# A decoder block on one core: the FFN factor spread by DMA, its squares between the high parts, and one attention product moved

## The reference

```
u = rms_norm(h, mix_norm_g);  proj = u @ w_in
o_attn = causal attention of 8 heads (dim 128) with a relative bias
o_ssm  = grouped rms_norm of a chunked scan, gated
o_mem  = attention of every token to 256 memory tokens, 4 heads (dim 256), keys and values = rms_norm(mem) @ w_mem_kv
merged = sum of sigmoid(gate) * (o_branch @ w_branch)
h = h + merged @ w_out
hid = causal_dwconv(rms_norm(h, ffn_norm_g) @ w_ffn_up, ffn_conv_w, ffn_conv_b)     # width 3
g_ff, up = split(hid)
out = rms_norm(h + (silu(g_ff) * up) @ w_ffn_down, final_norm_g)

rms_norm(x, g) = x * rsqrt(mean(x * x) + 1e-6) * g
```

## Time and profile before

| | us |
|---|---|
| median of 3 runs | 685.7 (685.39 to 686.08) |
| the profiled execution's own time | 685.14 |
| its span | 683.3 |
| PE busy | 673.6 |
| DVE busy | 493.9 |
| ACT busy | 370.2 |

### The profile page before, as it was taken

One profiled execution on the slowest core, in us unless ns is written; L12 is line 12 of the kernel. 1 busy time (PEld: TensorE's weight loads), 2 busy tenths in 40 slices (PEclk: granted clock), 3 DMA queues, 4 the chain that ended last, 5 costly groups with the idle time before them and its releaser, 6 DMA issues.

```text
span 683.3 us, 11411 instructions
## 1 busy us (share of the span) xinstructions
PE 673.6 (99%) x4505; PEld 616.5 (90%) x4505; DVE 493.9 (72%) x616; ACT 370.2 (54%) x461; POOL 9.9 (1%) x22
## 2 busy tenths in 40 slices
PE   8999999999999999999999999999999999999996
PEld 6999999999999988899888888888899999999995
DVE  6886979696866766777755655556688777777796
ACT  6668767767455544555533333443466555555552
POOL 0000000000100000000000000000000000000001
PEclk9999999999999999999999999999999999999998
DMA  9785767569195456545566665665436555555521
GB/s 297 236 266 172 247 202 257 159 223 326 62 265 175 144 164 232 173 150 168 170 218 215 217 191 182 196 229 173 169 124 207 186 185 187 188 185 186 193 82 62
DMA packets 99505, 130.92 MB, mean 192 GB/s; under 512 B 5649, under 2 KB 73742, under 8 KB 98830
## 3 DMA queue, kind: packets, MB, share of 16 engines
q1 hardware_dynamic: 97926, 125.27, 56.3%
q10 hardware_dynamic: 1544, 5.16, 2.1%
HBM read 129.31 MB, written 2.68 MB: 193 GB/s over the span
## 4 chain that ended last, share of the span: by engine, by line
PE 96%; DVE 1%; ACT 1%; DMA 1%; POOL 0%; issue 0%; POOLq 0%; SPq 0%; DVEq 0%; ACTq 0%
PE ps L364 30%; PE ps L365 30%; PE ps L366 30%; PE ps L674 1%; DMA x_nat<-x 1%; PE ps L711 1%; PE ps L659 1%; PE ps L419 1%; PE ps L675 1%; PE ps L694 1%; DVE w_lo L336 0%; DVE h_nat L1733 0%; PE ps L702 0%; PE ps L693 0%; ACT w_hi L332 0%; PE ps L713 0%
## 5 line engine op out<-in xcount | busy, mean ns | idle before, releaser
L336 DVE TENSOR_TENSOR w_lo<-w_raw,w_hi 128x2048 fp32r<-128x2048 f32 x107 | 244.6, 2287 | 90.8 <-ACT w_hi L332 90.8
L332 ACT ACTIVATE w_hi<-w_raw 128x2048 fp32r<-128x2048 f32 x107 | 204.3, 1910 | 100.7 <-PE ps L366 93.9
L364 PE MATMUL ps<-tok_hi,w_hi 128*128 128x256 f32 x864 | 247.0, 286 | 0.7 <-DVE tok_lo L1295 0.7
L365 PE MATMUL ps<-tok_lo,w_hi 128*128 128x256 f32 x864 | 244.5, 283 | 0.0
L366 PE MATMUL ps<-tok_hi,w_lo 128*128 128x256 f32 x864 | 244.5, 283 | 0.0
L364 PEld LDWEIGHTS ps<-tok_hi,w_hi 128*128 128x128 f32 x864 | 165.7, 192 | 2.3 <-issue 0.9
L365 PEld LDWEIGHTS ps<-tok_lo,w_hi 128*128 128x128 f32 x864 | 165.8, 192 | 0.4
L366 PEld LDWEIGHTS ps<-tok_hi,w_lo 128*128 128x128 f32 x864 | 165.7, 192 | 0.0
L364 PE MATMUL ps<-w_hi,tok_hi 128*128 128x512 f32 x128 | 50.2, 392 | 0.0
L365 PE MATMUL ps<-w_lo,tok_hi 128*128 128x512 f32 x128 | 49.9, 390 | 0.0
L366 PE MATMUL ps<-w_hi,tok_lo 128*128 128x512 f32 x128 | 49.8, 389 | 0.0
(11 more groups left out here) (266 smaller groups left out, 1000.7 us busy)
## 6 DMA issues: line engine op xcount, KB each, us to landing
w_raw<-w_in SPq DMA_DIRECT2D x94, 512.0 KB, 4.8
w_raw<-w_ffn_up SPq DMA_DIRECT2D x44, 512.0 KB, 4.4
w_raw<-w_ffn_down SPq DMA_DIRECT2D x22, 512.0 KB, 3.9
w_raw<-w_mem_kv SPq DMA_DIRECT2D x16, 512.0 KB, 4.5
w_raw<-w_br_ssm SPq DMA_DIRECT2D x16, 512.0 KB, 4.9
acs_b<-acs_d ACTq DMA_DIRECT2D x4, 1024.0 KB, 6.6
w_raw<-w_br_attn SPq DMA_DIRECT2D x8, 512.0 KB, 4.9
w_raw<-w_br_mem SPq DMA_DIRECT2D x8, 512.0 KB, 4.5
```

The lines of the kernel that those rows point to most:

```text
L332: act.activation(w_hi[:, s, :], w_raw[:, s, :], ACT.Copy).then_inc(hi_ready[s], 1)
L336: dve.tensor_tensor(w_lo[:, s, :], w_raw[:, s, :], w_hi[:, s, :].bitcast(F32), ALU.subtract).then_inc(lo_ready[s], 1)
L364: pe.matmul(o, a[0], b[0], start=start, stop=False, **kw)
L365: pe.matmul(o, a[0], b[1], start=False, stop=False, **kw)
```

## The change

- attend(4) leaves its place between gemm_cols(RC) and gemm_wide(RC) and goes between gate1_part(1) and turn_mem_probs(1). ACT's and DVE's copies of its output move with it, from step 0 to step 1 of the stage.
- The two spreading products, their bank and DVE's copy go. Instead ACT writes each half of stat to DRAM (128 rows of 4 bytes, two DMAs), does split_hi(RG, 0), waits for both, and reads the 256 factors back, broadcast to all partitions (128 KB), into rstd_b; DVE waits for that DMA ahead of its first pad_g.
- ACT's two squares move from behind h_high(3) to between h_high(1) and h_high(2), with waits of their own for the sums of h.

```diff
--- before.py
+++ after.py
@@ -232,6 +232,7 @@
     acs_d = nc.dram_tensor("acs_d", (SHEADS, T), F32, kind="Internal").ap()
     group_d = nc.dram_tensor("group_d", (GROUPS, T), F32, kind="Internal").ap()
     factor_d = nc.dram_tensor("factor_d", (GROUPS, T), F32, kind="Internal").ap()
+    h_factor_d = nc.dram_tensor("h_factor_d", (T,), F32, kind="Internal").ap()
     m_factor_d = nc.dram_tensor("m_factor_d", (T,), F32, kind="Internal").ap()
     bias_once = nc.dram_tensor("bias_once", (HEADS, BIAS_W), F32, kind="Internal").ap()
     bias_d = nc.dram_tensor("bias_d", (HEADS, P, BIAS_W), F32, kind="Internal").ap()
@@ -284,8 +285,8 @@
         sem, ("qm_low", "bias_g1_in", "sums_out", "gates_out", "gate_tanh_s", "gated_in", "mg_hi_s", "mg_lo_s"))
 
     out_done, h_added = sem("out_done"), sem("h_added")
-    h_sumsq, h_var, h_rstd, h_spread, rstd_b_ready, late_turned, h_hi, h_lo = map(
-        sem, ("h_sumsq", "h_var", "h_rstd", "h_spread", "rstd_b_ready", "late_turned", "h_hi", "h_lo"))
+    h_sumsq, h_var, h_rstd, h_factor_kept, rstd_b_in, late_turned, h_hi, h_lo = map(
+        sem, ("h_sumsq", "h_var", "h_rstd", "h_factor_kept", "rstd_b_in", "late_turned", "h_hi", "h_lo"))
     pads_zero, conv_begun, f_step, g_tanh, g_silu, hid_done, hid_hi_s, hid_lo_s = map(
         sem, ("pads_zero", "conv_begun", "f_step", "g_tanh", "g_silu", "hid_done", "hid_hi_s", "hid_lo_s"))
     down_done, y_added, y_gained, y_sumsq, y_var, y_rstd, y_first, y_left, y_right, y_out = map(
@@ -788,13 +789,14 @@
             turn_probs(4)
 
             gemm_cols(pe, RC, 1, me_hi, me_lo, tiles=(m_lo, 1))
-            attend(4)
             pe.wait_ge(oa_lo_s, 3)
             gemm_wide(pe, RC, 0, me_hi, me_lo)
             mem_scores(0)
             for i in range(1, 4):
                 gate1_part(i)
-                if i > 1:
+                if i == 1:
+                    attend(4)
+                else:
                     mem_attend(i - 1)
                 turn_mem_probs(i)
                 gemm_cols(pe, RC + i, 1, me_hi, me_lo)
@@ -902,12 +904,7 @@
                     mm = cols_part(pe, s, j, range(HK, KT), ps[:, s, j * T:(j + 1) * T], tok_hi, tok_lo, start=False,
                                    stop=False, skip_group_check=True)
                 mm.then_inc(gemm_done[s], 1)
-                if s == 1:
-                    pe.wait_ge(h_rstd, NT)
-                    for t in range(NT):
-                        mm = pe.matmul(ps[:, 3, t * P:(t + 1) * P], stat[:, 4 + t:5 + t].to_broadcast([P, P]), ident,
-                                       start=True, stop=True)
-                    mm.then_inc(h_spread, 1)
+
             def down(r, s, n, hi, lo, first=False):
 
                 pe.wait_ge(hid_lo_s, n)
@@ -1150,7 +1147,9 @@
                     act.wait_ge(group_kept, 48)
                     act.dma_start(rstd_g[:], factor_d.unsqueeze(0).to_broadcast([P, GROUPS, T])).then_inc(rstd_g_in, 16)
                 else:
-                    if i > 1:
+                    if i == 1:
+                        attended_hi(4)
+                    else:
                         mem_attended_hi(i - 1)
                     act.wait_ge(mp_turned, i)
                     act.activation(mprob_hi[:], halves(4), ACT.Copy).then_inc(mpt_hi_s, 1)
@@ -1162,8 +1161,6 @@
                     act.wait_ge(bank_free[0], r + 2)
                     at = g1[:, :, RW * (i // 2):RW * (i // 2 + 1)]
                     act.activation(at, at, ACT.Tanh, scale=0.5).then_inc(gate_tanh_s, 1)
-                if first:
-                    attended_hi(4)
                 act.wait_ge(norm_step, GT * i + GT)
                 act.activation(os_hi[:, bass.ds(GT * i, GT), :], o_tmp[:], ACT.Copy).then_inc(os_hi_s, 1)
                 if i % 2:
@@ -1219,12 +1216,22 @@
             split_hi(act, RF + 1, 0)
             split_hi(act, RF + 1, 1)
             split_hi(act, RF + 1, 2)
-            for c in range(4):
-                h_high(c)
+            h_high(0)
+            h_high(1)
+            act.wait_ge(bank_free[2], RF + 2)
             for t in range(NT):
+                act.wait_ge(h_added, 2 + t)
                 act.activation(h_sc[:, t, :], h_nat[:, t, :], ACT.Square,
                                accum_out=stat[:, 4 + t:5 + t]).then_inc(h_sumsq, 1)
+            h_high(2)
+            h_high(3)
+            for t in range(NT):
+                act.wait_ge(h_rstd, t + 1)
+                act.dma_start(h_factor_d[t * P:(t + 1) * P].rearrange("(p a) -> p a", a=1),
+                              stat[:, 4 + t:5 + t]).then_inc(h_factor_kept, 16)
             split_hi(act, RG, 0)
+            act.wait_ge(h_factor_kept, 16 * NT)
+            act.dma_start(rstd_b[:], on_all(h_factor_d, T)).then_inc(rstd_b_in, 16)
 
 
             def ffn(f, sa, na, sb, nb, after_gate, after_up, last, first=False, hi=hid_hi):
@@ -1529,6 +1536,8 @@
                 dve.wait_ge(qm_hi_s, i + 1)
                 dve.tensor_tensor(qm_lo[:], qm[:, 2 * i:2 * i + 2, :], qm_hi[:].bitcast(F32), ALU.subtract).then_inc(
                     qm_low, 1)
+                if i == 1:
+                    attended_lo(4)
                 if i > 1:
                     mem_attended_lo(i - 1)
                 if not first:
@@ -1547,7 +1556,6 @@
                 low(1, km_hi, km_lo, km_hi_s, i + 1, bank_free[1])
                 split_lo(dve, r + 1, 1)
                 if first:
-                    attended_lo(4)
                     dve.wait_ge(rstd_g_in, 16)
                 for c in range(GT):
                     dve.scalar_tensor_tensor(o_tmp[:, c, :], v_ssm[:, bass.ds(GT * i + c, 1), :].squeeze(1),
@@ -1672,9 +1680,7 @@
             h_low(2)
             h_low(3)
             split_lo(dve, RG, 0)
-            dve.wait_ge(h_spread, 1)
-            dve.tensor_copy(rstd_b[:], ps[:, 3, 0:T]).then_inc(rstd_b_ready, 1)
-            dve.wait_ge(rstd_b_ready, 1)
+            dve.wait_ge(rstd_b_in, 16)
             dve.wait_ge(pads_zero, 2)
```

## The result

The changed kernel takes 695.75 us (median of 4 runs, 694.91 to 696.87) where the kernel before takes 685.55 us beside it (4 runs): the recorded ratio is 1.0154, 95% interval 1.0142 to 1.0166 (the two medians alone give 1.0149). It is slower by 10.2 us, and the forecast range ended at 686.6. The profiled execution took 695.85 us with a span of 693.6, against 685.14 and 683.3 before, so the span grew by 10.3 us, and the trace says where.

What follows compares the result with a forecast made beforehand. PE, busy 99% of the span, was taken as the bound. Terms of -0.41 - 0.44 - 0.11 = -0.96 us, taken from the median of 685.70 us, gave 684.7 us, with a range from 684.1 to 686.6.

Steps and rivals of the forecast that it cites:

- Terms 1, 2 and 3: Savings on PE: attend(4) moved, 0.41 us; spreading products gone, 0.44 us; stall ahead of gemm_cols(RG, 1) gone, 0.11 us.
- rival 3: An entry of 0.3 us moves along with attend(4), leaving -0.55 us, 685.1 us; chance 0.15.
- the stall of the earlier trace: PE's weight load for gemm_cols(RG, 1) waits for DVE's split, 506.89 instead of about 506.77; 0.11 us lost.
- Step (b): DVE free of split_lo(RG, 0): squares fit ACT's idle at no cost; DVE's split ends at 497.8, 1.6 us earlier.
- Step (c): Factor on all partitions for pad_g: writes land at 495.6, broadcast takes 2.05 us, factor there at 497.7.
- The bound after it: Broadcast landing costs PE 1:1 from 499.2, makes a loss from 500.2, shows as slower from 501.5.
- the chain of 7.06 us: From pad_g's start to the end of DVE's split, awaited by PE at gemm_cols(RG, 1); said to have no slack.
- Rival 1: Writes and broadcast in turn become pad_g's last releaser: +1.7 us (687.4) or +4.8 us (690.5); chance 0.12.

Runs made afterwards that it cites:

- the two other slow kernels: Changed kernel with only the factor's first half written, adjacent, broadcast reading m_factor_d: by one DMA, 695.55 us; by eight DMAs of 16 pieces, 696.36 us.

## Why the prediction was wrong, by its own steps

**Terms 1, 2 and 3 were right.** Attend(4) takes 1.31 us at its new place (1.30 was said), and in the traces its move is worth 0.45 to 0.46 us, where 0.41 was said. It starts in step, 0.23 us behind the product ahead of it, so rival 3, an entry of its own, has nothing; and gemm_wide(RC) doesn't wait for oa_lo. The spreading products leave no gap, and the stall of the earlier trace rows is gone wherever pad_g is in time. With all three and no writes the kernel is 1.00 us faster, where the sum said 0.96; a match that close is partly luck, since the interval of that kernel runs from 0.4 to 1.6 us.

**Step (b) was right, and conservative.** The squares cost ACT nothing and the second half of the high parts started at 491.36, on its cue from PE. But I put the two issues in a row behind the high parts, where they run among them: split_hi(RG, 0) starts at 492.79, not at 493.6, and DVE's split ends at 497.05, not at 497.8.

**Step (c) failed**, and with it the forecast: the landing of the writes was taken as following their data. "The writes land half a microsecond behind the weights, 495.6" is right to the tenth for the last packet (495.54), and for writes of another form it is right for the landing as well (495.66 with the pieces 512 bytes apart, 495.39 in two rows). In the changed kernel the landing came 6.8 us later, at 502.4, though the second write was issued 1.3 us earlier than the prediction had it. This is the term that the sum had at nothing. The broadcast, priced at 1.73 + 0.3 = 2.05, is the smaller error of the step: it took 6.2, beside two weight loads that the writes had held up, and takes 2.9 to 3.1 where the writes were quick.

I had two kinds of rows for a small transfer: a read of 4 KB in 32-byte lines (1.73 us) and the write of nearly the same form, m_factor_d (6.6). I took the first and explained the second by the full queue beside it. That explanation was half right. In the trace before, m_factor_d's write is issued at 191.47, has its first packet at 195.19 and its last at 196.66, and lands at 198.05: 3.7 us pass before the first packet, beside the full queue, but 1.4 lie behind the last, much like the 1.6 of the kernel with 64 pieces of 8 bytes in each 512 bytes. The change packs twice as many pieces into each stretch, and there it is 6.9, so even the row of nearly the same form was no upper end. And "the queue is empty from 495.1" was true and worth nothing: the DMA engines are idle from 496 to 498 while the writes are still pending. The kernel before had a sign of the rest, too. Behind that write's landing the DMA engines were partly busy and moved next to nothing (stretch, busy time of the engines, clock, DMA share, GB/s):

```profile
198.00:199.00 1.00, 1.00 (x10) 1.00 (x10) 0.43 (x1) 0.51 (x1) 0.00 (x0) 1.00 0.39 19
199.00:200.00 1.00, 1.00 (x11) 1.00 (x10) 0.00 (x0) 1.00 (x1) 0.00 (x0) 1.00 0.47 82
```

**The bound after it held.** That a late landing "costs 1:1 from a landing at 499.2" is the mechanism that was measured, and the chain of 7.06 us came out to the hundredth (508.64 to 515.70). The kernel with 64 pieces shows it between the ends: pad_g at 502.57, a wait of 3.45 us on PE, +2.7 us in all (687.85 against 685.12).

**Rival 1 named the mechanism and the place, with the wrong price.** Its far end was a landing at 505.0 and +4.8 us; the landing was at 508.6. Of the 3.6 us between, the writes bring 3.6 (10.2 against 6.6) and the broadcast 1.0 (6.2 against 5.2), less 1.0 for the issue at 492.16 instead of 493.2. With the 1.47 us of the lower clock and the restart, which it didn't price, 4.8 + 3.6 + 1.5 = 9.9 of the 10.2 measured. Its reason, a row of nearly the same form, deserved more than 0.12.

**What was named as the sign of a wrong prediction** is what the trace shows: a landing past 499.2, and a new wait of PE on w_lo at gemm_cols(RG, 1).

## What to carry to other kernels

A column of one number per partition should not be written to memory as it stands: 128 pieces of 4 bytes in 512 bytes took 10 us to land here and slowed the transfers behind them, while one small product turned it into rows that landed in 3. Where a trace has a transfer of the same form as the one to be priced, take it apart before using it: what passes before the first packet was the queue here, what passes behind the last packet was the form of the write. A row that merely has the same size is no price. And an idle DMA engine is no sign that a write has landed: look at the semaphore's waiter, not at the traffic.

## What the hardware showed that was not expected

- The slow write holds up others. Behind 128 pieces in 512 bytes the two loads of 512 KB take 7.1 to 9.4 us, behind 64 they take 6.9, and 3.9 to 4.6 in the kernels whose writes are quick. In the changed kernel and the one with unused writes the traffic stays at 29 to 46 GB/s from 498 to 504, also past the landing. A broadcast issued behind such a write takes 4.6 to 6.2 us instead of 2.9 to 3.1; it shares the engines with the late loads then, and how much of it is due to them wasn't separated.
- A pending write may leave no trace of itself: its last packet is recorded at 495.54, from 496 to 498 us the DMA share is 0.00, and the landing comes at 502.39.
- A stall of PE can cost more than its length. Behind the wait of 9.41 us the clock was granted at 0.52 from 516 to 519, and products stood 0.21 us apart until 518.91, and behind the waits of 8.15 and 9.22 us in the two other slow kernels it was granted at 0.50 with products 0.21 us apart until 519 or later; behind the wait of 3.45 us in the kernel with 8-byte pieces the granted clock was 1.00 all along, and the products were 0.12 us apart two starts later.
- Eight DMA issues on ACT's queue keep ACT from its next activation for 2.7 to 2.8 us, some 0.5 us for each from the third on.
